# Second block's hybrid mixer: dilated attention moved beside the input projection, and its RMS factors on eight numbers per token

## The chip, the core and the metric

The kernel runs on one NeuronCore of one Trainium2 chip. The metric is the device time of one execution in microseconds (us). Everything is in float32; products that need it are made from a rounded high part and a low part of each operand.

## The reference, cut to what matters

Two model blocks run one after the other over 512 tokens of width 1024. The second block's mixer takes the normed input `h`, projects it, and feeds two mixers whose outputs are joined and projected back:

```python
def hybrid_mixer(h, w_in, gate_bias, g_q, g_k, g_mh, w_out):
    proj = h @ w_in                      # mq, mk, mv, mo, mg, aq, ak, av
    hm = bidirectional_mlstm(mq, mk * 64 ** -0.5, mv, gates of mg)      # 4 heads, both directions
    hm = rms_norm(hm, g_mh) * sigmoid(mo)
    qa = partial_rope(rms_norm(aq, g_q), pos) * 64 ** -0.5              # 8 heads of 64
    ka = partial_rope(rms_norm(ak, g_k), pos)
    ha = dilated_attention(qa, ka, av)   # three bands, dilations 1, 4, 16, merged by their log-sum-exp
    return concatenate([hm, ha]) @ w_out
```

The kernel makes the three bands as one softmax whose weights are multiplied by a table `CM` (how many of the three bands hold a key) and masked by a table `CB`.

## The kernel before, in words

A program is a list of steps. Each engine walks the list in the order in which the steps were added and issues the part that the step has for it, with semaphore waits in front. So on every engine an instruction that waits holds back all that was added behind it. The order of the list is written by hand, with Python generators that are advanced by turns.

`mixer_hybrid` has three stages.

**Projection.** `w_in_2` is taken in 25 chunks of 128 columns (`MQ` 2, `MK` 2, `MV` 4, `MO` 4, `MG` 1, `DQ` 4, `DK` 4, `DV` 4; `D` is the dilated attention, `M` the mLSTM). A chunk is 24 dense matmuls of 512 tokens (`ProjMM`, function `dense`, L192 to L194) into one PSUM bank. ACT copies the bank out (`Evac`). The next chunk's weights are split into a high part on ACT (L179) and a low part on DVE (L184) meanwhile. Small follow-up steps of earlier chunks are generators in the list `lag`; after each chunk's matmuls each of them is advanced by one part. For a `DQ` or `DK` chunk (`normed_rope`, class `NormedRope`) the parts are: square on ACT; a TensorE product with a block of ones that puts each head's sum of squares on all its 64 partitions (L2194), a root on ACT (L2209), a reciprocal of 128x512 on DVE (L2216) and the scaling (L2219); then the rotation (L2198 and three DVE operations); then the split into high and low parts (`HiLo`). A `DV` or `MV` chunk is turned to token-major (`Turn`, L1187). The gate chunk `MG` starts the gates of the mLSTM, and then eight `MlBroadcast` steps (L2431, L2432) which put a running maximum on all partitions, copied by ACT into `MB` (L2439). `MO` chunks leave their bank through a Sigmoid.

**Two mixers side by side.** After `Begin` the generators `mlstm` and `dilated` are advanced by turns.

`dilated` treats 16 pairs `q`, a pair being two heads and 128 queries, in the order (query block, head pair). Its steps for a pair are: `DilScore` (six score matmuls and two mask matmuls into banks 4 and 5, then on DVE a maximum per bank, L2806, then on ACT an Exp per bank into `PP`, L2816); `DilCount` (DVE multiplies with `CM` and sums, L2837); twice `DilTrans`, once for each bank of the pair (four transposes into a bank, L2858, and the copy of that bank by ACT into `PT`, L2865); `DilPV` (L2888). After four pairs come `DilDen` and `DilQuot` (L2937), the division. `DilTrans` takes its PSUM bank so:

```python
        self.b = 3 if u % 2 and 3 in w.ptfree else 6
        self.bankfree = w.ptfree[self.b]
```

and `w.ptfree` holds only bank 6 until the mLSTM gives bank 3 away, late.

`mlstm` treats 16 units (head, key block): `MlExp` (four Exps on ACT, and the three matmuls of the scores, L2505 to L2507), `MlProd` (two multiplications on DVE, L2529), `MlSum` (L2555, L2560). Behind the units comes a chain of small steps: `MlDen`, `MlInverse`, `MlSpread`, `MlQuot`, `MlSquare`, `MlRoot`, `MlRootInverse`, `MlFactor`, `MlOut`, and `MixSplit` of each head, in which DVE, ACT and TensorE hand work to each other.

**Output projection.** `out_products`, with the same dense matmuls on the split mixer output.

Of the kernel before, what the change touches and what calls it, by code (L numbers as in the profile page):

```python
# [1072 lines left out]
class ProjMM(Step):  # L1073


    def __init__(self, pr, parts):
        self.pr, self.parts = pr, parts
        one = len({p.ch for p in parts}) == 1
        self.order = [(p, k) for p in parts for k in range(8)] if one else [
            (p, k) for at in (0, T) for k in range(8) for p in parts if p.c0 == at]  # L1080
        for p, k in self.order:
            if k == 7:
                p.done = p.u.used = pr.P.s["group"].next()
# [155 lines left out]
class Mix:  # L1239


    def __init__(self, MIX, MH, ML):
        self.MIX, self.MH, self.ML = MIX, MH, ML
        self.hi, self.lo, self.order = {}, {}, []


class MixSplit(Step):
# [8 lines left out]
    def scalar(self, act):  # L1256
# [3 lines left out]
        for k in self.ks:  # L1260
            act.e.activation(mix.MH[:, k, :], mix.MIX[:, k, :], ACT.Copy).then_inc(mix.hi[k].sem, 1)

    def vector(self, dve):
        mix = self.mix
        for k in self.ks:
            dve.wait_ge(*mix.hi[k])
            dve.e.tensor_tensor(mix.ML[:, k, :], mix.MIX[:, k, :], mix.MH[:, k, :].bitcast(F32),
# [3 lines left out]
class OutMM(Step):  # L1271
# [11 lines left out]
    def tensor(self, pe):  # L1283
# [4 lines left out]
        for i, k in enumerate(ms.order):  # L1288
            pe.wait_ge(*ms.hi[k])
            pe.wait_ge(*ms.lo[k])  # L1290
            dense(pe, self.P.banks[self.b], u, slice(k * 128, (k + 1) * 128), (ms.MH[:, k, :], ms.ML[:, k, :]), True,
# [872 lines left out]
class NormedRope(Step):  # L2164


    def __init__(self, pr, part, st, tiles):
# [5 lines left out]
        elif part == 1:  # L2173
            self.b, self.free = pr.sidebank()
            self.rsfree = tiles.rsfree
            st["sum"] = tiles.sqfree = s["side_mm"].next()
            st["root"] = pr.sidefree[self.b] = s["nr_act"].next()
            st["inv"] = s["rope"].next()
            st["scaled"] = tiles.rsfree = s["rope"].next()
# [8 lines left out]
    def tensor(self, pe):  # L2188
        P, st, ti = self.P, self.st, self.tiles
        if self.part == 1:  # L2190
# [9 lines left out]
    def scalar(self, act):  # L2200
# [5 lines left out]
        elif self.part == 1:  # L2206
            act.wait_ge(*st["sum"])
            act.wait_ge(*self.rsfree)
            act.e.activation(ti.RS, P.banks[self.b], ACT.Sqrt, scale=1.0 / 64, bias=P.EPSC).then_inc(st["root"].sem, 1)  # L2209

    def vector(self, dve):
        P, st, ti = self.P, self.st, self.tiles
        x = st["x"]
        if self.part == 1:
            dve.wait_ge(*st["root"])
# [3 lines left out]
            dve.e.scalar_tensor_tensor(x, x, st["gain"], ti.RS, ALU.mult, ALU.mult).then_inc(st["scaled"].sem, 1)  # L2219
        elif self.part == 2:  # L2220
# [9 lines left out]
class RopeTiles:  # L2230
    def __init__(self, SQ, RS, TM, RT, PR, landed, gained):
        self.SQ, self.RS, self.TM, self.RT, self.PR, self.landed, self.gained = SQ, RS, TM, RT, PR, landed, gained
        self.sqfree = self.rsfree = self.tmpfree = NONE
# [15 lines left out]
class Mlstm:  # L2249


    def __init__(self, P, Q, K, V, O, G, UT, OH, MIX, lent, kept):
# [9 lines left out]
        room = lambda places: [P.over_ring(f"ROOM{i}{part}", [128, 2, T], F32, part + i * 4096)[:, half, :]  # L2262
                               for i in places for part in (0, NUNIT * 4096) for half in range(2)]
        self.MB, kept = room(lent), room(kept)
# [9 lines left out]
    def tiles(self, ctx, QH, QL, KH, KL):  # L2274
# [3 lines left out]
        self.A = sb("A", [128, 4, T])  # L2278
        self.RH = sb("RH", [36, T], F32R)
# [134 lines left out]
class MlBroadcast(Step):  # L2414


    def __init__(self, m, pr, h, d):
        self.m, self.h, self.d = m, h, d
        self.b, self.free = pr.sidebank()
        self.split = m.mgsplit  # L2420
        self.spread = m.P.s["side_mm"].next()
        self.done = pr.sidefree[self.b] = m.P.s["ml_act"].next()
# [11 lines left out]
    def scalar(self, act):  # L2434
        m = self.m
        act.wait_ge(*self.spread)
        for t in m.lent:
            act.wait_ge(*t)
        act.e.activation(m.MB[self.d * 4 + self.h], m.P.banks[self.b], ACT.Copy).then_inc(self.done.sem, 1)  # L2439
# [288 lines left out]
class MlOut(Step):  # L2728
# [8 lines left out]
    def vector(self, dve):  # L2737
# [4 lines left out]
        dve.wait_ge(*self.scaled)  # L2742
# [1330 lines left out]
```

## Time and profile before

| what | us |
|---|---|
| median of 3 runs | 3217.79 (3216.38 to 3219.81) |
| span of the profiled execution, first to last instruction | 3213.4 |
| TensorE busy in it | 3123.6 (97%) |
| VectorE busy | 1911.2 (59%) |
| ScalarE busy | 1046.4 (33%) |
| mean granted TensorE clock | 0.985 of 2.4 GHz |

The profile gives the span of its execution and no other time of it; what lies around the span is inside the runs' time only. An engine's busy time hides its waits, so the stages are read one by one: the projection is 2465 to 2628 us of the span, the two mixers side by side 2629 to 2792 us, and the dense matmuls of the output projection start at 2792 us. The matmuls' ends are modelled, so the distance from one start to the next is the better duration.

### The profile page before, as it was taken

To read this page: it belongs to the slowest core of one execution; us is meant where nothing else is said; L and a number is where in the kernel's file an instruction comes from. 1 tells how busy PE (TensorE), PEld (TensorE's weight loads), DVE (VectorE), ACT (ScalarE), POOL (GpSimd) and SP (SyncE) were. 2 spreads that over 40 slices of the span, in tenths; PEclk is the share of its full clock that TensorE was granted. 3 is DMA by queue.
4 is the path that set the end of the run, shared out by engine and by line. 5 is a ranking of instruction groups with operands and counts; after the bars stand their busy time and mean duration, and the time that the engine had idled before them with its cause. 6 is when DMAs were issued, how large, how long until landed. Compare 5 with 4: busy or idle time off the path is not lost.

```text
span 3213.4 us, 37101 instructions
## 1 busy us (share of the span) xinstructions
PE 3123.6 (97%) x15003; PEld 2512.4 (78%) x15014; DVE 1911.2 (59%) x2753; ACT 1046.4 (33%) x1516; POOL 10.2 (0%) x23
## 2 busy tenths in 40 slices
PE   8999999998899999999999999999999998899998
PEld 7888888776678888788877888788887764578887
DVE  7876555645675554766657554566665565574444
ACT  4212222335442222422235222332224444442222
POOL 0000000000000000000000000000000000000000
PEclk9999999999999999999999999999999999899999
DMA  6433332210033443256532443235551220133231
GB/s 231 141 118 127 147 126 81 68 46 11 2 132 127 158 153 131 79 192 214 196 107 79 150 158 138 79 118 202 185 189 59 78 59 1 47 119 104 92 99 53
DMA packets 102996, 369.21 MB, mean 115 GB/s; under 512 B 11374, under 2 KB 12670, under 8 KB 102572
## 3 DMA queue, kind: packets, MB, share of 16 engines
q1 hardware_dynamic: 101788, 362.14, 33.0%
q0 software_dynamic: 1040, 4.71, 0.4%
q8 instruction: 120, 1.97, 0.3%
q14 instruction: 48, 0.39, 0.0%
HBM read 364.71 MB, written 2.10 MB: 114 GB/s over the span
## 4 chain that ended last, share of the span: by engine, by line
PE 88%; DVE 7%; ACT 3%; issue 1%; DMA 1%; SPq 0%; POOL 0%; DVEq 0%; ACTq 0%; POOLq 0%
PE ps L192 25%; PE ps L194 25%; PE ps L193 25%; PE ps L196 4%; PE ps L197 2%; DVE SQ L614 1%; PE ps L499 1%; DVE WL L184 1%; DVE HL L603 1%; DVE XT L1037 1%; DVE RAW L1499 0%; PE ps L2888 0%; PE ps L2858 0%; PE ps L2788 0%; PE ps L2555 0%
## 5 line engine op out<-in xcount | busy, mean ns | idle before, releaser
L192 PE MATMUL ps<-HH,WH 128*128 128x512 f32 x2400 | 945.3, 394 | 4.0 <-ACT S L914 2.2
L194 PE MATMUL ps<-HH,WL 128*128 128x512 f32 x2400 | 935.1, 390 | 0.0
L193 PE MATMUL ps<-HL,WH 128*128 128x512 f32 x2400 | 934.5, 389 | 0.0
L179 ACT ACTIVATE WH<-RAW 128x1024 fp32r<-128x1024 f32 x456 | 459.2, 1048 | 632.0 <-PE ps L194 361.8
L184 DVE TENSOR_TENSOR WL<-RAW,WH 128x1024 fp32r<-128x1024 f32 x456 | 542.8, 1220 | 73.5 <-ACT WH L179 73.2
L192 PEld LDWEIGHTS ps<-HH,WH 128*128 128x128 f32 x2400 | 450.7, 188 | 107.5 <-issue 9.5
L193 PEld LDWEIGHTS ps<-HL,WH 128*128 128x128 f32 x2400 | 450.9, 188 | 95.2 <-issue 3.8
L194 PEld LDWEIGHTS ps<-HH,WL 128*128 128x128 f32 x2400 | 450.5, 188 | 95.4
L1037 DVE SCALAR_TENSOR_TENSOR XT<-ps,DER,XT 128x512 f32<-128x512 f32 x512 | 346.6, 683 | 246.6 <-PE ps L194 231.8
L192 PE MATMUL ps<-GH,WH 128*128 128x512 f32 x1056 | 414.1, 392 | 4.8 <-DVE GL L945 4.8
L194 PE MATMUL ps<-GH,WL 128*128 128x512 f32 x1056 | 411.2, 389 | 0.0
L193 PE MATMUL ps<-GL,WH 128*128 128x512 f32 x1056 | 411.0, 389 | 0.0
L943 DVE TENSOR_TENSOR S<-S,ps 128x512 f32<-128x512 f32 x128 | 88.0, 687 | 513.9 <-PE ps L194 513.9
L918 ACT ACTIVATE GH<-S 128x512 fp32r<-128x512 f32 x128 | 80.9, 632 | 625.2 <-DVE S L943 625.2
L305 DVE SCALAR_TENSOR_TENSOR DUMP<-RAW,CC 128x1024 bf16<-128x1024 f32 x200 | 244.4, 1222 | 12.4 <-DVE DUMP L305 0.5
L192 PEld LDWEIGHTS ps<-GH,WH 128*128 128x128 f32 x1056 | 198.2, 188 | 49.9 <-issue 7.5
L194 PEld LDWEIGHTS ps<-GH,WL 128*128 128x128 f32 x1056 | 198.2, 188 | 42.0
L193 PEld LDWEIGHTS ps<-GL,WH 128*128 128x128 f32 x1056 | 198.4, 188 | 39.3 <-issue 0.7
L196 PE MATMUL ps<-HC,WH 128*128 128x512 f32 x424 | 152.1, 399 | 0.0
L945 DVE TENSOR_TENSOR GL<-S,GH 128x512 fp32r<-128x512 f32 x128 | 88.6, 693 | 97.0 <-ACT GH L918 97.0
L914 ACT ACTIVATE S<-ps 128x512 f32<-128x512 f32 x128 | 76.0, 594 | 201.8 <-PE ps L194 201.6
L197 PE MATMUL ps<-HC,WL 128*128 128x256 f32 x424 | 118.8, 280 | 0.0
(382 smaller groups left out, 2627.0 us busy)
## 6 DMA issues: line engine op xcount, KB each, us to landing
RAW<-in_w_modt SPq DMA_DIRECT2D x200, 512.0 KB, 5.0
RAW<-in_ffn_wi SPq DMA_DIRECT2D x182, 512.0 KB, 5.0
RAW<-in_w_gu SPq DMA_DIRECT2D x90, 512.0 KB, 4.5
RAW<-in_ffn_wo SPq DMA_DIRECT2D x88, 512.0 KB, 4.6
RAW<-in_w_in SPq DMA_DIRECT2D x44, 512.0 KB, 3.6
RAW<-in_w_down SPq DMA_DIRECT2D x44, 512.0 KB, 4.2
RAW<-in_w_out SPq DMA_DIRECT2D x16, 512.0 KB, 4.5
STG<-in_w_modt SPq DMA_DIRECT2D x10, 512.0 KB, 12.7
```

What stands on the lines that cost most here:

```text
L179: act.e.activation(u.hi, u.ld.view, ACT.Copy).then_inc(u.hi_done.sem, 1)
L184: dve.e.tensor_tensor(u.lo, u.ld.view, u.hi.bitcast(F32), ALU.subtract).then_inc(u.lo_done.sem, 1)
L192: pe.e.matmul(out, wh, x[0], start=first, stop=False)
L193: pe.e.matmul(out, wh, x[1], start=False, stop=False)
L194: m = pe.e.matmul(out, wl, x[0], start=False, stop=last)
L196: pe.e.matmul(out, wh, x, start=first, stop=True, skip_group_check=not first)
L197: m = pe.e.matmul(out[:, 0:TC], wl, x[:, 0:TC], start=False, stop=True, skip_group_check=True)
L305: dve.e.scalar_tensor_tensor(self.dump, self.view, 1.0, tile[:, :], ALU.mult, ALU.mult, accum_out=self.P.DOT[:, self.row % 2, j, self.f:se ...
L918: act.e.activation(gh, s, ACT.Copy).then_inc(self.hi[n].sem, 1)
L943: dve.e.tensor_tensor(s, s, F.SX[:, :] if n else out, ALU.mult).then_inc(self.mul[n].sem, 1)
L945: dve.e.tensor_tensor(gl, s, gh.bitcast(F32), ALU.subtract).then_inc(self.lo[n].sem, 1)
L1037: dve.e.scalar_tensor_tensor(x, o, P.mod_g(F.mi, d, j), x, ALU.mult, ALU.add).then_inc(w.evac[d, n][i].sem, 1)
```

## The change

- The order of the projection's chunks becomes, for i = 0 to 3, `DQ+i`, `DK+i`, `DV+i` and `MG` (i = 0) or `MV+i-1`; then `MV+3`, `MQ`, `MK`, and `MO` last.
- `projection` gets a hook, `between`: after each chunk but the first two (which are made as one job) it advances the generator `dilated` two times. `dilated` waits, in the list, until `DQ` and `DK` of its head pair are split.
- The 16 pairs are ordered (head pair, query block). The steps of a pair come in another order, in two pieces: `DilScore(q)`, `DilTrans(2q-2)`; then `DilDen`, `DilTrans(2q-1)`, `DilPV(q-2)`, `DilQuot`, `DilCount(q)`. Both pieces stand right behind each other in the projection.
- The projection has two banks instead of four (0, 1) and two side banks (2, 3); the attention keeps 4 to 7, and `w.ptfree` holds bank 6 alone.
- `NormedRope` has four parts. The sums of squares are taken as [128 tokens, 8] by four matmuls with two moving columns each; ACT takes Ln and Exp of these 8 numbers per token (half the exponent negated), DVE refines them by three small operations, and eight matmuls with a broadcast stationary operand spread them to a bank, from which the scaling reads. The 3.35 us reciprocal is gone. `LogExpTable` loads one activation table set ahead.
- The eight `MlBroadcast` steps leave the projection and stand at the start of `mlstm`, on banks 0 to 2. The sigmoid of `MO` becomes a step `MlSigmoid` behind `MlDen`.
- What is left beside `mlstm` is `dilated_end`: the `MixSplit` of the four dilated chunks.

```diff
@@ class NormedRope: tensor, scalar, vector @@
-            pe.e.matmul(P.banks[self.b], ti.PR[:, 128:256], ti.SQ, start=True, stop=True).then_inc(st["sum"].sem, 1)
+            for n in range(4):
+                m = pe.e.matmul(P.banks[self.b][:, 2 * n:2 * n + 2], ti.SQ[:, n * 128:(n + 1) * 128], ti.PR[:, 128:256:64],
+                                start=True, stop=True)
+            m.then_inc(st["sum"].sem, 1)
         elif self.part == 2:
+            pe.wait_ge(*st["inv"])
+            pe.wait_ge(*self.free)
+            for n in range(4):
+                for h in range(2):
+                    rs = ti.RS[:, st["at"], 2 * n + h:2 * n + h + 1].broadcast_to([128, 64])
+                    m = pe.e.matmul(P.banks[self.b][64 * h:64 * h + 64, n * 128:(n + 1) * 128], rs, P.ID, start=True,
+                                    stop=True, skip_group_check=True)
+            m.then_inc(st["spread"].sem, 1)
+        elif self.part == 3:
...
-            act.e.activation(ti.RS, P.banks[self.b], ACT.Sqrt, scale=1.0 / 64, bias=P.EPSC).then_inc(st["root"].sem, 1)
+            act.e.activation(r, P.banks[self.b][:, 0:8], ACT.Ln, scale=1.0 / 64, bias=P.EPSC).then_inc(self.ln.sem, 1)
+            act.wait_ge(*self.ln)
+            act.e.activation(r, r, ACT.Exp, scale=-0.5).then_inc(st["root"].sem, 1)
...
-            dve.e.reciprocal(ti.RS, ti.RS).then_inc(st["inv"].sem, 1)
-            dve.wait_ge(*st["inv"])
+            dve.e.scalar_tensor_tensor(v, ss, EPS * 64, r, ALU.add, ALU.mult).then_inc(self.prod.sem, 1)
+            dve.wait_ge(*self.prod)
+            dve.e.scalar_tensor_tensor(v, v, -0.5 / 64, r, ALU.mult, ALU.mult).then_inc(self.half.sem, 1)
+            dve.wait_ge(*self.half)
+            dve.e.scalar_tensor_tensor(r, v, 1.5, r, ALU.add, ALU.mult).then_inc(st["inv"].sem, 1)
@@ class Program: projection @@
                     evac(p)
+                    if len(chs) == 1 and between:
+                        between()
+                        between()
@@ mixer_hybrid @@
-                pr = Proj(self, h, (0, 1, 2, 3), (4, 5, 6, 7))
+                pr = Proj(self, h, (0, 1), (2, 3))
...
-                order = [DQ, DV, MG, DV + 1, DQ + 1, DV + 2, DV + 3, DQ + 2, MQ, MQ + 1, DQ + 3, MK, MK + 1]
+                order = []
                 for i in range(4):
-                    order += [DK + i, MV + i]
-                order += list(range(MO, MG))
-                self.projection(pr, a["w_in_2"], order, lambda ch: [(0, T)], evac, lag)
+                    order += [DQ + i, DK + i, DV + i, MG if i == 0 else MV + i - 1]
+                order += [MV + 3, MQ, MQ + 1, MK, MK + 1] + list(range(MO, MG))
+                self.projection(pr, a["w_in_2"], order, lambda ch: [(0, T)], evac, lag, between=lambda: next(steps, None))
@@ dilated @@
         for q in range(last + 2):
-            if 1 <= q <= last:
-                self.add(DilCount(w, q - 1))
             if q < last:
+                while w.pairs[q][0] not in w.qsplit or w.pairs[q][0] not in w.ksplit:
+                    yield
                 self.add(DilScore(w, q))
-                yield
             if 1 <= q <= last:
                 self.add(DilTrans(w, 2 * q - 2))
-                yield
+            yield
+            if 1 <= q <= last:
                 if q % 4 == 0:
                     self.add(DilDen(w, q // 4 - 1))
                 self.add(DilTrans(w, 2 * q - 1))
...
                 self.add(DilPV(w, q - 2))
                 if q % 4 == 1:
                     self.add(DilQuot(w, q // 4 - 1))
-                yield
+            if q < last:
+                self.add(DilCount(w, q))
+            yield
@@ mlstm @@
         split(0)
-        yield
+        done = [NONE] * 3
+        for h in range(4):
+            for d in range(2):
+                done.append(self.add(MlBroadcast(m, h, d, done[-3])).done)
+            if h % 2:
+                yield
...
         self.add(MlDen(m, last.done))
+        self.add(MlSigmoid(m))
```

## Rows read from the trace of the kernel before

**Rows 1.** Busy time by stage; columns: stretch, length, PE, PEld, DVE, ACT, POOL, granted clock

```profile
2465.10:2628.20 163.10, 162.43 (x684) 123.13 (x684) 101.87 (x101) 69.34 (x99) 3.15 (x6) 1.00 0.27 79
2629.10:2704.95 75.85, 69.56 (x338) 32.29 (x344) 40.39 (x86) 42.05 (x95) 0.00 (x0) 1.00 0.00 1
2704.95:2792.20 87.25, 67.85 (x399) 39.44 (x404) 54.59 (x110) 35.79 (x60) 0.00 (x0) 0.78 0.09 29
```

**Rows 2.** Timeline of ACT, evacuations of the projection's last two chunks

```profile
2622.80 0.60 ACT L1131 ACTIVATE MIX<-ps 128x512 f32<-128x512 f32 x1 [3.89 <-PE ps L194]
2628.24 0.60 ACT L1131 ACTIVATE MIX<-ps 128x512 f32<-128x512 f32 x1 [4.84 <-PE ps L194]
```

**Rows 3.** Timeline of all engines, one step of the attention (start, length)

```profile
2742.45 0.49 PE L2788 MATMUL ps<-KH,QH 64*128 64x512 f32 x2
...
2744.07 1.02 PE L2673 MATMUL ps<-A,OH 128*4 128x512 f32 x2
2744.18 1.29 DVE L2806 TENSOR_REDUCE NM<-ps 128x1 f32<-128x512 f32 x2 [2.02 <-PE ps L2788]
2744.91 1.29 ACT L2816 ACTIVATE PP<-ps,NM 128x512 f32<-128x512 f32 x2 [1.48 <-DVE NM L2806]
2745.03 1.09 PE L2858 MATMUL ps<-K,PP 128*128 128x128 f32 x8
...
2746.05 1.09 PE L2888 MATMUL ps<-PT,DVt 128*64 128x128 f32 x16
2746.09 1.08 ACT L2865 ACTIVATE PT<-ps 128x512 f32<-128x512 f32 x2
```

**Rows 4.** Chain of waits, projection: one product with the ones

```profile
2604.20 0.86 PE ps L2194 x2
```

**Rows 5.** Timeline of PE: one broadcast in the projection; the nearest to two-column sums

```profile
2515.73 0.49 PE L2431 MATMUL ps<-MGH,SEL 4*128 4x512 f32 x1
...
2516.38 0.66 PE L1187 MATMUL ps<-K,SQ 128*128 128x128 f32 x4
...
2821.64 0.50 PE L764 MATMUL ps<-K,ACC 128*128 128x1 f32 x4
2822.01 0.47 PE L192 MATMUL ps<-MH,WH 128*128 128x512 f32 x1
```

**Rows 6.** Groups by line, both stages (count, then busy us, mean ns, idle before)

```profile
L2216 DVE RECIPROCAL TMP<-TMP 128x512 f32<-128x512 f32 x8 | 26.8, 3353 | 24.4 <-ACT TMP L2209 24.4
...
L2209 ACT ACT_TABLE_LOAD x2 | 2.6, 1283 | 0.0
...
L2937 PE MATMUL ps<-XT,K 128*64 128x512 f32 x16 | 4.8, 605 | 0.4 <-DVE XT L2913 0.4
...
L2602 DVE RECIPROCAL G<-G 36x128 f32<-36x128 f32 x4 | 3.8, 946 | 0.1
L2640 DVE TENSOR_TENSOR ROOM<-ROOM,ps 128x512 f32<-128x512 f32 x8 | 5.1, 680 | 0.0
```

**Rows 7.** Timeline of PE: one unit of the mLSTM, from its scores to the next work

```profile
2666.95 0.49 PE L2505 MATMUL ps<-MQH,MKH 64*128 64x512 f32 x1
...
2670.08 0.50 PE L2788 MATMUL ps<-KH,QH 64*128 64x512 f32 x2
```

**Rows 8.** Timeline of DVE: one head's output steps and its split, twice

```profile
2776.99 0.69 DVE L1267 TENSOR_TENSOR ML<-MIX,MH 128x512 fp32r<-128x512 f32 x1 [1.27 <-ACT MH L1261]
...
2779.76 0.69 DVE L1267 TENSOR_TENSOR ML<-MIX,MH 128x512 fp32r<-128x512 f32 x1 [0.69 <-ACT MH L1261]
```

**Rows 9.** Timeline of PE: starts behind an idle stretch (length in brackets)

```profile
1306.68 1.11 PE L713 MATMUL ps<-SA,K 128*128 128x512 f32 x1 [2.02 <-DVE SA L417]
...
2706.84 0.63 PE L2858 MATMUL ps<-K,PP 128*128 128x128 f32 x4 [1.90 <-ACT G L2585]
```

**Rows 10.** Busy time and granted clock of the stretches behind those two

```profile
1307.20:1310.50 3.30, 3.30 (x8) 1.96 (x7) 3.30 (x5) 1.89 (x3) 0.00 (x0) 0.54 0.14 21
...
2706.84:2710.00 3.16, 3.00 (x27) 1.84 (x28) 2.28 (x6) 0.60 (x1) 0.00 (x0) 1.00 0.02 5
```

More of the change, by code:

```diff
@@ L1242, in __init__ @@
     def __init__(self, MIX, MH, ML):
-        self.MIX, self.MH, self.ML = MIX, MH, ML
+        views = lambda t: t if isinstance(t, list) else [t[:, k, :] for k in range(8)]
+        self.MIX, self.MH, self.ML = MIX, views(MH), views(ML)
         self.hi, self.lo, self.order = {}, {}, []
@@ L2414, with __init__ @@
 class MlBroadcast(Step):
[L2417 to L2422, printed above, removed]
+    def __init__(self, m, h, d, before):
+        self.m, self.h, self.d, self.b = m, h, d, (2 * h + d) % 3
+        self.split, self.free = m.mgsplit, before
+        self.spread = m.P.s["ml_mm"].next()
+        self.done = m.P.s["ml_act"].next()
         m.bcast[h, d] = self.done
@@ L2434, in scalar, with __init__ @@
     def scalar(self, act):
+        m, h = self.m, self.h
+        act.wait_ge(*self.spread)
+        act.e.activation(m.MB[self.d * 4 + self.h], m.P.banks[self.b], ACT.Copy).then_inc(self.done.sem, 1)
+class MlSigmoid(Step):
+    def __init__(self, m):
+        self.m = m
+        m.opened = [m.P.s["ml_gate"].next() for _ in range(4)]
+    def scalar(self, act):
         m = self.m
[L2436 to L2439, printed above, removed]
+        for h in range(4):
+            act.e.activation(m.O[:, h, :], m.O[:, h, :], ACT.Sigmoid).then_inc(m.opened[h].sem, 1)
 class MlMask(Step):
@@ L2815, in scalar @@
                 act.wait_ge(*w.trans[u - 4].turned)
-            act.e.activation(w.PP[:, u % 4, :], w.P.banks[4 + par], ACT.Exp,
+            else:
+                for t in w.freed:
+                    act.wait_ge(*t)
+            act.e.activation(w.PP[u % 4], w.P.banks[4 + par], ACT.Exp,
                              bias=w.NM[:, s, hs:hs + 1]).then_inc(self.exp[par].sem, 1)
@@ L2872, in __init__ @@
         self.w, self.q = w, q
-        self.n, self.j = w.pairs[q]
-        self.ready = [w.trans[2 * q + par].done for par in range(2)]
+        self.j, self.n = w.pairs[q]
+        self.ready = [w.trans[2 * q + par].done for par in range(2)] + [w.turned[self.j]]
         self.done = w.P.s["dil_mm"].next()
@@ L3326, in follow, with projection @@
         lag.append(g)
-    def projection(self, pr, w, chunks, segs_of, evac, lag, beside=None, depth=1):
+    def projection(self, pr, w, chunks, segs_of, evac, lag, beside=None, depth=1, between=None):
         def job(chs):
@@ L3848, in dilated, with dilated_end @@
                     self.add(DilQuot(w, q // 4 - 1))
-                yield
+            if q < last:
+                self.add(DilCount(w, q))
+            yield
+    def dilated_end(self, w, steps, mix):
+        for _ in steps:
+            yield
+        for k in range(4, 8):
+            self.add(MixSplit(self, mix, [k], [w.quot[k - 4].done]))
+            yield
     def plan(self):
```

173 lines of the change are left out of this document (96 added, 77 removed).

## The prediction

> **What bounds the kernel now.** I read the busy time by stage first [rows 1]. In the projection TensorE is busy 162.4 of 163.1 us at full clock: a chunk costs what its matmuls cost, and the reader is to see that ACT (69 us) and DVE (102 us) have room there. In the two stretches of the mixers TensorE is idle 6.3 of 75.9 us and then 19.4 of 87.3 us, and the granted clock of the second is 0.78. So the place where there is something to win is the second stretch, 2705 to 2792 us, and everything that the change sends into the projection costs its full TensorE time, since nothing there is free. A dense chunk is 5.44 us from one evacuation to the next [rows 2].
>
> **The attention's matmuls, moved.** They cost TensorE the same wherever they stand. From the start of one step's scores to what follows is 1.62 us (2742.45 to 2744.07), the transposes of both banks of a pair take 1.02 us (2745.03 to 2746.05), and the product with V 1.02 us (eight matmuls; half of the row's records would be 0.5) [rows 3]. The divisor's spread is at most 4.8 us for all four [rows 6]. Sum: 16 x 1.62 + 16 x 1.02 + 16 x 1.02 + 4.8 = 63.3 us more in the projection. The list shows where they fall: `DQ`, `DK` of head pair 0 are split at the sixth chunk, pair q = 0 starts there, the splits of the later head pairs are ready at chunks 9, 13 and 17 (counted from 0), exactly when q = 4, 8, 12 ask for them, so there is one pair per chunk without a hole and q = 17 ends two chunks before the end. All 63.3 us lie in the projection.
>
> **A new wait inside each step.** This is the term that decides. Follow one step behind a chunk. TensorE: scores of q, transposes of 2q-2 into bank 6, transposes of 2q-1 into bank 6 again, product q-2, next chunk. The second transposes wait until ACT has copied bank 6 away. But ACT's list has, before that copy, the two Exps of q, these wait for the two maxima of q on DVE, and these for the scores of q. In the rows of one step [rows 3] the scores end at 2744.07, the maxima start at 2744.18, the Exps at 2744.91, and the first copy can only start at 2746.09, behind them. It takes about 0.54 us (half of 1.08), so bank 6 is free at about 2746.7. The first transposes would be over at 2744.07 + 0.51 = 2744.6. TensorE would stand still for 2.1 us. Before the change the two `DilTrans` of a pair were added a turn apart, with mLSTM matmuls in between (0.95 us of them stand in this row, before the transposes), and the Exps of a pair a turn earlier still. After it, both pieces of the step stand right behind each other and behind the still waiting transposes stand the product and the whole next chunk. q = 1 to 15 have this wait: 15 x 2.1 = 31.5 us. In six of these chunks DVE still has a rotation and a turned chunk to copy before the maxima, which makes the wait some 0.5 us longer: 3.0 us. For q = 16 there are no scores and only the copy is waited for, 0.7 us. Sum 35.2 us. Bounds: nothing, if something hides it, and 50 us (3.3 us per step) if DVE and ACT are found busy with the weights' split each time.
>
> Who else waits: `DilCount` is behind the Exps on DVE and ends in the next chunk, before the next transposes need it. The split of the next chunk's weights is added before a chunk's matmuls and has the 5.4 us of that chunk; it is not late. ACT's copies and Exps, moved, add 16 x (1.29 + 1.08) us to a 69 us load, DVE's maxima and counts about as much: neither becomes the bound, each chunk now lasting about 11 us.
>
> **Norm factors.** The reciprocals, 26.8 us of DVE [rows 6], and their roots lie beside the matmuls: they cost nothing now, but for one wait of 0.7 us at the second chunk (163.1 less 162.4). On TensorE: eight products of 0.86 us go, 6.9 us [rows 4]. For the sums of squares (four float32 matmuls, eight records, two columns) the nearest row is 0.37 us for four records with one column [rows 5], so 0.74 us each, 5.9 us in all (0.37 if they pair up: 3.0). The spread is eight matmuls of 128 columns on half the array's width, like the product with V [rows 3]: 1.02 us each, 8.2 us (at best half, 4.1). The eight broadcasts leave: 0.65 us each [rows 5], 5.2 us. Sum: -6.9 + 5.9 + 8.2 - 5.2 - 0.7 = +1.3 us. The small operations on ACT and DVE (under 0.3 us each) have a chunk's time each. The new second side bank is enough: no part waits for a bank that a slower one of the same chunk holds for more than 0.3 us. The weight loads on SP's queue and the tables on POOL's are the same in number; a chunk lasts longer than before, so they come no later.
>
> In a sentence of its own: the Trainium skill, "ScalarE: Activation LUTs", section "Table sets: the hidden batching unit", says that one set holds both Exp and Ln, so the preloaded set should serve the whole projection; no row here shows it. If it did not, loads would come back into ACT's list, and that is the fourth rival below.
>
> **The mLSTM alone.** One unit costs TensorE 3.13 us from start to start of what follows [rows 7]; units with less wide sums cost 0.2 less, so 3.0. DVE (two products, a quarter of the masks) and ACT (four Exps) need less than 2 us each, and a unit's exponentials only wait for the sums two units before, so TensorE sets the pace. The start: splits of q and k, eight broadcasts whose copies take 0.6 us each on ACT, two splits of `dilated_end` between them, two masks, the first Exps and products: 11.2 us (estimate, 8 to 13) until the first sum. Then 15 x 3.0 + 1.5 for four heads' changes + 2.1 for the last sum. 59.8 us. The chain behind it: floor and denominator on ACT 1.9 (the idle stretch before 2706.84 [rows 9]); four inverses, 3.8 [rows 6] and 1.0 for their maxima; split and first spread 2.5; twelve DVE operations of 0.64 (5.1/8 [rows 6]), 7.8; square, its sum, root, refinement, split and the first factor 8.8, of which the filler matmuls at low clock are a part; four heads at 2.77, each with the turn to ACT and back [rows 8], 11.1; the split of the first output weights 1.6. Sum 38.5 us (30 to 42). `MlSigmoid` lies beside the inverses. Together 98.3 us, against 2792.2 - 2628.2 = 164.0 before: -65.7 us. The clock: TensorE idles for most of the chain and at the start, and where before the clock rose just before the output matmuls it will now be low when they begin. 3.5 us (0 to 7). So -62.2 us.
>
> **The clock in the projection.** The question is whether idle stretches of 2.1 to 2.7 us let it fall. Behind the 2.02 us stretch that ends at 1306.68 the granted clock is 0.54 of 2.4 GHz for 3.3 us, though dense matmuls go on; behind 1.90 us it stays at 1.00 [rows 9, 10]. In the whole trace, idle stretches of TensorE between 1.6 and 1.9 us never lowered it when matmuls stood around them (six), and those between 1.99 and 2.6 us did in six cases of seven. 2.1 us is just beyond the boundary. I take 10 of 15 steps, each with 3.4 us at 1.2 GHz, in which half is lost: 17 us (0 to 51, the latter if each falls and takes twice as long to rise, as it did in the stage of small matmuls).
>
> The Trainium skill, "TensorE: Matmul & The Clock Gate", section "HAM oscillation — how this bites in real kernels", would let only idle gaps clearly longer than these lower the clock. By that rule the 17 us would be 0. The row of 1306.68 disagrees, and I go by the row; the rule is the second rival.
>
> **Sum.** +63.3 + 35.2 + 1.3 in the projection, -62.2 behind it, +17 of clock = +54.6 us. On the profile's span of 3213.4 us that is 3268.0. The runs' median lies 4.4 us above the span, for what is around it; it moves with it: 3217.8 + 54.6 = 3272.4, I say 3272 us.
>
> **Rivals.**
>
> First, the other side: the wait for bank 6 is hidden, a step costs only its matmuls, and the clock holds. Then the sum is 54.6 - 35.2 - 17 = +2.4, and -12 with the terms that have a low end there (spreads -4.1, sums of squares -2.9, start -3.2, clock behind the stage -3.5). About 3213 us. It decides from the point where a step's idle is under about 0.1 us. For it: ACT has room and the copy is short. Against it: the order in ACT's list is fixed, and the rows of one step show each link [rows 3].
>
> Second: the wait is there but the clock holds: 54.6 - 17 = +37.6, 3255 us. For it: the 1.90 us stretch, only 0.2 shorter. Against it: the 2.02 us one.
>
> Third: nearly every step loses the clock, and for longer, because scores and products use half of the array or less: 17 becomes some 45, 3300 us.
>
> Fourth, that the set loaded ahead does not stay: a load (1.3 us [rows 6]) before some Exps, on the very chain that TensorE waits for, for the eight chunks in which a Ln stands: +10 us, 3282 us.
>
> **Chances.** The forecast 0.48; hidden wait 0.12; clock holds 0.20; third 0.12; fourth 0.05; something else at the start or in the chain, slower still, 0.03. Below the range lies nearly all of the first rival, above it part of the third: 3238 to 3300. A measurement of this kernel can tell about 0.2%, 6.4 us, from no change. Of the first rival somewhat more than half lies below that: faster 0.07, same 0.05, all the rest slower, 0.88.
>
> **What would show it.** In the changed kernel: each pair of transposes from q = 1 on in two groups with some 2.1 us of TensorE idle between them, released by ACT's copy; ACT's Exps waiting for DVE's maxima in each step; a chunk pitch of 11 to 12 us from the sixth chunk on; projection about 263 us plus the clock; granted clock below 1.00 in patches there; from the last projection matmul to the first output matmul about 100 us. No reciprocal of 128x512. If the two groups of transposes stand together, or if the pitch is near 9.5 us, I am wrong at the second term; if the wait is there and the clock reads 1.00, at the last.

## The result, and the profile after

The changed kernel takes 3280.09 us (median of 4 runs, 3277.9 to 3284.87), the kernel before 3217.11 us on the same chip (4 runs, 3216.38 to 3219.81). The ratio is 1.0199, 95% interval 1.0186 to 1.0211: 63 us slower. The profiled execution has a span of 3278.4 us and a mean granted clock of 0.980.

Busy time by stage, as in [rows 1]; first the projection, then the mLSTM alone, up to the first matmul of the output projection:

```profile
2468.30:2753.75 285.45, 248.62 (x1356) 181.20 (x1372) 128.50 (x229) 98.28 (x163) 3.15 (x6) 0.94 0.17 53
2753.75:2855.05 101.30, 75.56 (x236) 31.63 (x237) 50.52 (x90) 48.59 (x103) 0.00 (x0) 0.79 0.00 0
```

The projection is 122.3 us longer (285.4 against 163.1), the part behind it 62.7 us shorter (101.3 against 164.0). TensorE, which had 0.7 us of idle time in the projection before, now shows 36.8 us (285.45 less 248.62). The waits of TensorE in that stage name the reason (engine and line, what it waited for, us in all, times, longest):

```profile
PE ps L2906 <- ACT ROOM L2913: 33.6, 16, 2.5
PE ps L2840 <- issue: 2.5, 16, 0.2
PE ps L2202 <- ACT TMP L2224: 0.6, 1, 0.6
```

L2906 is the transposes, L2913 the copy of bank 6. The row with "issue" is no stop of TensorE: L2840 is the two mask matmuls of each pair, and of these 32 the trace holds 16 records. In r1 below, whose trace holds all 32, the second one starts 0.66 us behind the scores' first record, exactly as the recorded one does here, and no such row appears. So the real idle time is 34.3 us.

One step of the attention, all engines, against [rows 3]:

```profile
2719.76 0.39 PE L2833 MATMUL ps<-KH,QL 64*128 64x512 f32 x2
2720.09 0.66 PE L2906 MATMUL ps<-K,ROOM 128*128 128x128 f32 x4
2720.20 1.29 DVE L2851 TENSOR_REDUCE NM<-ps 128x1 f32<-128x512 f32 x2 [6.88 <-PE ps L2833]
2720.93 1.28 ACT L2864 ACTIVATE ROOM<-ps,NM 128x512 f32<-128x512 f32 x2 [1.77 <-DVE NM L2851]
...
2722.11 0.59 ACT L2913 ACTIVATE ROOM<-ps 128x512 f32<-128x512 f32 x1
...
2722.84 0.63 PE L2906 MATMUL ps<-K,ROOM 128*128 128x128 f32 x4 [2.10 <-ACT ROOM L2913]
```

Read it from the top: scores end, maxima start 0.1 us later, the Exps 0.7 us after that, and the copy, ready to run since the first transposes ended at 2720.7, starts at 2722.11, behind the Exps in ACT's list. The second transposes stand 2.10 us. Twelve steps show 2.09 or 2.10 us, three show 2.54, and the last one 0.83. Before, the same pair of transposes stood in one row without a gap [rows 3].

The granted clock behind three of these waits (ending at 2566.70, 2722.84 and 2554.18):

```profile
2566.70:2570.10 3.40, 3.40 (x22) 2.70 (x23) 2.01 (x6) 1.54 (x2) 0.00 (x0) 0.55 0.00 0
2723.70:2727.10 3.40, 3.40 (x21) 2.75 (x18) 1.98 (x4) 1.35 (x2) 0.00 (x0) 0.54 0.00 0
2554.20:2557.60 3.40, 3.40 (x28) 2.75 (x29) 1.28 (x4) 2.06 (x3) 0.00 (x0) 1.00 0.02 5
```

0.55 and 0.54 are the lower level, 1.2 GHz; 22 and 21 matmul records fit in where 28 do at 1.00. Ten of the fifteen steps have such a patch, 34 us in all, so 17 us are lost.

Lines of the new norm factors (groups; count, busy us, mean ns, idle before) and the one table load of the stage:

```profile
L2211 PE MATMUL ps<-K,RS 128*64 128x128 f32 x128 | 8.7, 279 | 0.0
L2202 PE MATMUL ps<-PR,TMP 128*128 128x2 f32 x64 | 8.1, 249 | 0.6 <-ACT TMP L2224 0.6
```

```profile
L2270 ACT ACT_TABLE_LOAD x1 | 1.3, 1283 | 0.0
```

And the waits of TensorE in the mLSTM alone, the two largest:

```profile
PE ps L192 <- ACT WH L179: 10.7, 1, 10.7
PE ps L2667 <- DVE RL L1209: 7.9, 1, 7.9
```

### The profile page after: what moved, and what is told of

Same layout as the page of the kernel before. It is cut to its first block, busy times and chain, and to the rows that moved or that the text cites. A ratio compares the mean times of both kernels' runs of the same rounds, so it can differ in the third digit from the quotient of the medians.

```text
span 3278.4 us, 37495 instructions
## 1 busy us (share of the span) xinstructions
PE 3148.0 (96%) x15174; PEld 2527.6 (77%) x15190; DVE 1890.1 (58%) x2769; ACT 1040.8 (32%) x1522; POOL 10.2 (0%) x23
## 4 chain that ended last, share of the span: by engine, by line
PE 86%; DVE 8%; ACT 4%; issue 1%; DMA 1%; SPq 0%; POOL 0%; DVEq 0%; ACTq 0%; POOLq 0%
PE ps L192 24%; PE ps L193 24%; PE ps L194 24%; PE ps L196 4%; PE ps L197 2%; DVE SQ L614 1%; PE ps L2936 1%; DVE WL L184 1%; DVE HL L603 1%; PE ps L2602 1%; ACT ROOM L2864 1%; PE ps L499 1%; DVE XT L1037 0%; DVE RAW L1500 0%; DVE DUMP L305 0%
```

## The experiments

Stages are compared by their lengths: from the projection's first dense matmul to its last, from there to the first output matmul, and from there to the end of the span. The projection's first matmul lies between 2463.1 and 2468.3 us in the traces of all these kernels, though nothing differs before it, so a stage's length says more than a span. All in us, worked out from the start and end of those matmuls:

| kernel | projection | mixers behind it | both | rest |
|---|---|---|---|---|
| before | 163.1 | 164.0 | 327.1 | 421.2 |
| changed | 285.4 | 101.3 | 386.7 | 423.4 |
| r1 scores last | 240.6 | 99.2 | 339.8 | 423.0 |
| r2 filler | 269.9 | 100.3 | 370.2 | 423.1 |
| r3 norm alone | 172.4 | 164.6 | 337.0 | 421.2 |
| r4 two banks | 256.2 | 100.2 | 356.4 | 423.1 |
| r5 four in the chain | 220.0 | 126.1 | 346.1 | 423.1 |
| r6 four in the units | 218.4 | 125.5 | 344.0 | 422.8 |
| r7 wide norm | 237.6 | 101.4 | 339.0 | 424.6 |
| r8 three in the chain, wide norm | 217.7 | 118.6 | 336.3 | 424.0 |
| r9 wide, pairs first | 229.7 | 99.5 | 329.3 | 424.3 |
| r10 narrow, pairs first | 243.9 | 102.3 | 346.2 | 423.0 |
| r11 fillers | 229.7 | 108.1 | 337.8 | 422.3 |
| r12 turn later, fillers | 225.2 | 101.9 | 327.2 | 422.6 |

**r1: the order within a step.** The changed kernel with the scores behind both transposes, so that the copy stands ahead of the Exps in ACT's list. The product with V moves too, from behind the second transposes to between the two:

```diff
+            while q < last and (w.pairs[q][0] not in w.qsplit or w.pairs[q][0] not in w.ksplit):
+                yield
-            if q < last:
...
-                self.add(DilScore(w, q))
             if 1 <= q <= last:
                 self.add(DilTrans(w, 2 * q - 2))
-            yield
+            if q >= 2:
+                self.add(DilPV(w, q - 2))
             if 1 <= q <= last:
                 self.add(DilTrans(w, 2 * q - 1))
...
+            yield
+            if q < last:
+                self.add(DilScore(w, q))
```

> The changed kernel with the attention's steps in another order: first transposes, product with V, second transposes, then the scores; the work is the same. Theory A (the second transposes wait for ACT's copy of bank 6, which stands behind the Exps of the scores, and the idle stretch lowers the clock): TensorE's 33.6 us of waits for that copy go to under 3 us, the granted clock in the projection is 1.00, 3229 us (3222 to 3240). Rival B (the attention's chain through DVE and ACT is too long for one chunk in any order): the wait appears somewhere else, time stays above 3265.

Measured: 3229.07 us (3226.9 to 3235.25), ratio 1.0042 (1.0028 to 1.0056). TensorE's waits for the copy fall from 33.6 to 2.8 us and the lower clock in the projection from 34.1 to 6.8 us: 30.8 + 13.7 = 44.5 of the 46.9 us by which the two stages are shorter. By the medians 51 of the 63 us of loss are this one order. No run parts its two moves. The last step of the changed kernel has no scores, and its second transposes wait 0.83 us with no product between; 15 steps like that would be 12 us (estimate), so the later scores bring most of the gain and the product between the transposes the rest.

**r2: the wait filled.** The changed kernel with four matmuls of 128x256, results unused, ahead of each pair's second transposes:

```diff
...
+        if self.u % 2:
+            pe.wait_ge(*self.fill)
+            for _ in range(4):
+                pe.e.matmul(P.banks[self.fb][:, 0:256], P.ID, P.K[:, 0:256], start=True, stop=True)
         pe.wait_ge(*self.bankfree)
```

> The changed kernel with four filler matmuls (1.7 us) on a free side bank before the second transposes of each pair; they change no result. Theory A, its second half (the lowered clock costs 17 us by itself): the wait stays, filled, and the clock stays 1.00 in the projection: 3263 us (3258 to 3268). Rival (the low patches cost nothing, because other things are waited for in them): 3278 to 3284, whatever the clock reads.

Measured: 3259.93 us (3258.89 to 3261.51), ratio 1.0135 (1.012 to 1.015). A step of it on TensorE, and the projection's clock:

```profile
2518.56 1.89 PE L2909 MATMUL ps<-K 128*128 128x256 f32 x8
2520.73 0.66 PE L2912 MATMUL ps<-K,ROOM 128*128 128x128 f32 x4 [0.28 <-ACT ROOM L2919]
```

```profile
PE ps L2912 <- ACT ROOM L2919: 4.4, 15, 0.3
```

The second transposes start 2.66 us behind the first (2.75 in the changed kernel), so nearly as late, but TensorE works until then, and no patch of the lower clock is left in the projection. It is 15.5 us shorter, against the 17 us that the patches cost; of the 20.1 us between the two spans 3.3 are only an earlier start of the stage. So the clock term is separate from the wait and about as large as said.

**r3: the norm factors alone**, put into the kernel before (the `NormedRope` and `LogExpTable` of the diff, nothing else).

> The kernel before with nothing of the change but the norm factors on eight numbers per token (four parts of NormedRope, one table set loaded ahead). My sum, with the sizes of the profile after: eight sums at 0.9 us and eight spreads at 1.0 in place of eight products of 0.86 us, 0.7 us of a wait gone: +8 us, 3225 us (3221 to 3229). Rival (the reciprocals' 27 us of DVE were felt somewhere): at or under 3217.

Measured: 3224.62 us (3220.29 to 3228.99), ratio 1.0022 (1.0013 to 1.0031). The projection:

```profile
2463.85:2636.29 172.44, 171.77 (x860) 133.70 (x860) 79.17 (x117) 63.33 (x104) 3.14 (x6) 1.00 0.24 75
```

It is 9.3 us longer, with DVE's load down from 102 to 79 us: the change relieves an engine that nobody waited for and pays on the one that is full.

**r4: two banks for the transposes**, in the changed kernel's own order. One of the two side banks goes to them:

```diff
-        self.ptfree, self.ofree = {6: NONE}, NONE
+        self.ptfree, self.ofree = {6: NONE, 3: NONE}, NONE
...
-                pr = Proj(self, h, (0, 1), (2, 3))
+                pr = Proj(self, h, (0, 1), (2,))
```

> The changed kernel, its order of steps kept, with bank 3 given to the second transposes and only bank 2 left to the side products of the projection. Theory A: the second transposes start at once, no wait for the copy; the side products now wait for each other's bank in three chunks of four, about 13 us in all; clock 1.00: 3242 us (3232 to 3252). Rival (it is not the bank but the late copy itself that holds TensorE, in the product with V): no gain, above 3270.

Measured: 3246.24 us (3244.34 to 3247.1), ratio 1.0091 (1.0076 to 1.0106). The wait for the copy is gone, others came in its place, all for the one side bank that is left:

```profile
PE ps L2202 <- DVE MIX L2248: 4.2, 4, 1.4
PE ps L1187 <- DVE DKt L2248: 3.7, 4, 0.9
PE ps L2211 <- DVE TMP L2253: 3.5, 4, 0.9
PE ps L1187 <- DVE TMP L2253: 2.6, 3, 0.9
```

That is 14.0 us. 33.6 - 14.0 = 19.6, and 10.2 us of clock (34.1 less 13.7 us at the lower level, halved): 29.8 of the 30.3 us that the stages gave back.

**r5 and r6: four pairs left where TensorE has holes.** r1, with the hook advancing the attention only 30 times; the four pairs of the last head pair run beside the chain behind the last unit (r5), or beside the units (r6: no turns held back).

```diff
+                early = (next(steps, None) for _ in range(30))
...
-                self.projection(pr, a["w_in_2"], order, lambda ch: [(0, T)], evac, lag, between=lambda: next(steps, None))
+                self.projection(pr, a["w_in_2"], order, lambda ch: [(0, T)], evac, lag, between=lambda: next(early, None))
@@ dilated_end, ahead of the rest of steps: the first two splits, and 16 turns held back (none in r6) @@
+        for k in range(4, 6):
+            self.add(MixSplit(self, mix, [k], [w.quot[k - 4].done]))
+            yield
+        for _ in range(16):
+            yield
...
```

> Kernel: the order of r1 (scores last in a step), and the four pairs of head pair 3 (q = 12 to 15) are not run beside the projection but beside the chain behind the mLSTM's last unit, where TensorE idles (40 us long from the last sum to the first output matmul in the changed kernel, TensorE busy for about a quarter). Theory A (matmuls moved into the projection cost their full time; those beside the chain are free as long as the chain doesn't wait for them): the projection gets 4 x 3.9 = 15.8 us shorter, the chain gets longer by about half of that, since its small DVE and ACT steps wait for the Exps and counts of the pairs: 3229 - 15.8 + 8 = 3221 us, 3214 to 3228. Rival B (the chain is held up by each pair as long as the pair's own maxima, Exps, counts and copies on DVE and ACT take, 4.9 us per pair): 3229 - 15.8 + 4 x 4.9 = 3233 us.

> As r5, but the four pairs run beside the mLSTM's units, where TensorE is itself the bound (2.9 to 3.1 us per unit). Theory A: TensorE's time is only moved from one full stage to another, so about the same as r1, 3229 us (3224 to 3234). Rival B (a unit leaves TensorE idle between its parts, which pairs would fill): 3215 us or less. If A holds and r5 is below r6, then where a pair stands decides, by whether TensorE idles there.

Measured: r5 3236.95 us (3233.65 to 3240.45), ratio 1.0062 (1.0048 to 1.0075); r6 3234.71 us (3231.91 to 3237.1), ratio 1.0055 (1.0041 to 1.0069). My theory was wrong for both. In r5 the projection got 20.6 us shorter, but the stage behind it 26.9 us longer. More than four pairs' work had moved: a pair is spread over three steps, and the trace has the scores of four pairs, the transposes of five and the products with V of six behind the projection, in r6 too. That is why the projection gained more than the 15.8 us expected. What it cost is still more than it gained, by 6.3 us; the rival had said 3.8. The wait of 7.9 us in the chain was not filled but replaced:

```profile
PE ps L2906 <- DVE ROOM L2885: 11.1, 4, 5.0
PE ps L2552 <- DVE A L2576: 2.2, 1, 2.2
```

L2885 is the multiplication with `CM`: a pair is itself a chain over DVE and ACT, and with nothing else between its parts TensorE waits for each. The 11.2 us before the output matmuls stayed as well, since no pair was left by then. r6 gained 22.2 us in the projection and paid 26.3 us for the same work; 5.1 us of it are waits for the copy of bank 6. Without them its theory, that work between two full stages is only moved, would have held.

**r7: the norm factors wide.** r1 with one product with the ones, Ln and Exp on 128x512, and the three refinements on 128x512; `V` shares its place with the rotation's temporary.

```diff
-            for n in range(4):
-                m = pe.e.matmul(P.banks[self.b][:, 2 * n:2 * n + 2], ti.SQ[:, n * 128:(n + 1) * 128], ti.PR[:, 128:256:64],
-                                start=True, stop=True)
+            pe.e.matmul(P.banks[self.b], ti.PR[:, 128:256], ti.SQ, start=True, stop=True).then_inc(st["sum"].sem, 1)
...
-            dve.e.scalar_tensor_tensor(x, x, st["gain"], P.banks[self.b], ALU.mult, ALU.mult).then_inc(st["scaled"].sem, 1)
+            dve.e.scalar_tensor_tensor(x, x, st["gain"], r, ALU.mult, ALU.mult).then_inc(st["scaled"].sem, 1)
```

> Kernel: the order of r1, and the norm factors not on 8 numbers per token: one product with the ones (0.86 us), Ln and Exp on 128x512, and the three refinements on 128x512 on DVE. Taken away from TensorE: four two-column sums (0.91 us in the changed kernel) and the eight-matmul spread (1.02 us), of each of the eight chunks: 8 x (0.91 + 1.02 - 0.86) = 8.6 us. Theory A (the norm part costs TensorE's time, and nothing else): 3229 - 8.6 = 3220.5 us, 3217 to 3225. Rival B (the narrow form is worth what it costs, because three wide operations of about 0.7 to 1.3 us on DVE per chunk hold up the attention's maxima and the weights' low part): 3229 us or slower.

**r8: r5 and r7 together.**

> r5 and r7 together. Theory A (the two gains lie in different stages and add up): r5 - 8 us, about 3213 us, that is a little faster than the kernel before (3217.5). Rival B (they overlap, or the wide operations on DVE hold up the chain): as r5, 3221 us, no faster than before.

Measured: r7 3227.68 us (3227.24 to 3229.66), ratio 1.0035 (1.0022 to 1.0047); r8 3229.21 us (3228.04 to 3231.43), ratio 1.004 (1.0027 to 1.0052). r7 was to gain 8.6 us and gained 3.0 in the projection. Of r7, TensorE in the projection:

```profile
PE ps L2889 <- ACT ROOM L2896: 9.3, 6, 2.7
```

The wait for the copy is 6.5 us more than in r1: the wide Ln and Exp, and the wide operations on DVE, stand ahead of it. With it both theories hold a part: the narrow form costs TensorE about 9 us, and the wide one gives most of that back through the order of the lists. r8 is 7.7 us faster than r5, but it isn't r5 and r7 added up. The wide form has one part less, so the splits are ready earlier, and the same 30 advances get one pair further: the trace has 13 pairs' scores in the projection (r5: 12) and three behind it. Of the 9.8 us between the two traces' stages 7.5 lie in the mixers' stage, which differs by that pair alone. So r8 says nothing on whether the two gains add up.

**r9 and r10: the attention's pieces first.** Behind a chunk's matmuls the two pieces of the attention's step, then the small follow-up steps and the evacuation; r9 with the wide norm factors (r7), r10 with the narrow ones (r1).

```diff
+                    if len(chs) == 1 and between:
+                        between()
+                        between()
                     if p.c0 == 0:
                         self.advance(lag)
                     evac(p)
-                    if len(chs) == 1 and between:
-                        between()
-                        between()
```

> r7 (scores last in a step, wide norm factors), and in addition the two pieces of the attention's step stand ahead of a chunk's small follow-up steps (norm, turns, rotation) and of its evacuation, not behind them. Theory A (in r7 the Ln and Exp of 128x512 on ACT and the wide operations on DVE stand ahead of the first transposes' copy and of the maxima, and this is what TensorE's 10 us of idle are): the idle goes to under 1 us, 9 us less, and with it the clock patches of 6.8 us, 3.4 us less: 3227.7 - 12.4 = 3215 us (3212 to 3220), a little faster than the kernel before. Rival B (the wait only changes its place: the follow-up products on TensorE now wait for ACT and DVE behind the Exps): 3225 to 3230 us.

> The same order with the narrow norm factors of the change (r1 with the pieces ahead of the follow-up steps). Theory A: r1's 3.4 us of idle and 3.4 us of clock go: 3229.1 - 6.8 = 3222 us (3219 to 3226); against r9 it then shows what the narrow form costs TensorE when nothing waits: 7 us (8.6 by the records' durations). Rival B (the spread, now further behind the Exps on ACT, waits): 3229 us or more.

Measured: r9 3219.45 us (3217.5 to 3225.26), ratio 1.0011 (1.0002 to 1.002); r10 3236.95 us (3236.79 to 3237.63), ratio 1.0062 (1.0048 to 1.0076). r9 came near its expectation, r10 missed it by 15 us. The stage of r9, and what TensorE waited for in r9 and in r10:

```profile
2464.17:2693.91 229.74, 222.94 (x1181) 160.33 (x1196) 140.65 (x229) 104.71 (x163) 3.14 (x6) 0.99 0.21 66
```

```profile
PE ps L1187 <- DVE UT L2431: 3.0, 1, 3.0
...
PE ps L2889 <- ACT ROOM L2896: 0.8, 1, 0.8
```

```profile
PE ps L1187 <- DVE TMP L2253: 4.3, 2, 2.1
...
PE ps L2211 <- DVE UT L2448: 1.9, 1, 1.9
```

In r9 the copy's wait went, and one new wait came where three side products share two banks. The narrow form has a product more per chunk, so it meets that wait more often. r10's projection is 14.2 us longer than r9's: 9.3 us is left when the waits (7.0 and 3.8 us) and the lower clock (6.8 and 3.4 us, halved) are taken out. That is r3's figure again. r10's own expectation had the waits going to nothing; they rose from 2.8 to 7.0 us instead.

**r11 and r12: fillers in the chain.** r11 is r9 with 28 matmuls of 128x256 behind the last sum and 38 behind the last factor; r12 has 16 and 23, and the turn of the running maxima one chunk later.

```diff
                     self.add(MlMax(m))
                     yield
+                    yield
...
         self.add(MlSigmoid(m))
+        self.add(Busy(self, 16, bank=4))
...
+            if h == 3:
+                self.add(Busy(self, 23, bank=4))
```

> r9, and filler matmuls of 128x256 (0.24 us each at full clock) in the two long idle stretches of the chain behind the mLSTM: 28 behind the last sum (idle 7.9 us) and 38 behind the last factor (idle 10.7 us); their results are not used. Theory A (in that chain the granted clock is low for about 17 and 14 us behind these two stretches, and spreads, squares and the first output matmuls run at half speed because of it): the clock holds, spreads and squares take half of their 12 us less what DVE needs anyway, 4 to 6 us, and the first output matmuls 2.3 us: 8 us faster than r9, 3207 us (3204 to 3212). Rival B (DVE and ACT set the pace of the chain, the clock does not matter there): as r9, or some us slower where fillers run past the idle.

> r9 with two additions. First, the turn of the gates' running maxima (three side products fall into its chunk, on two banks, and TensorE waits 3.0 us there, with a clock patch of 3.4 us behind it) comes one chunk later, where one product fewer is. Second, the fillers of r11 at the size that the idle stretches have: one of them took 0.44 us in r11 (28 of them 12.35 us), not 0.24, so 16 behind the last sum (7.0 of 7.9 us) and 23 behind the last factor (10.1 of 11.2 us). Theory A (a wait removed in a full stage comes back whole with its clock patch; fillers that end before the chain does cost nothing and keep the clock for the squares' sums, 2.9 us, and the first output matmuls, 2.4 us): 3219.5 - 3.0 - 1.7 - 2.9 - 2.4 = 3209.5 us (3207 to 3214), 0.2% faster than the kernel before. Rival B (DVE and ACT set the chain's pace, so the fillers give nothing, and the wait for the turn moves to the next chunk): 3217 to 3220 us, no different from before.

Measured: r11 3229.02 us (3226.32 to 3229.69), ratio 1.0036 (1.0022 to 1.005); r12 3215.74 us (3213.65 to 3219.11), ratio 0.9997 (0.9988 to 1.0006). In r11 I had taken half of a filler's price; of r11 and then of r12:

```profile
2755.88 12.35 PE L499 MATMUL ps<-K 128*128 128x256 f32 x56
```

```profile
2768.64 6.22 PE L2703 MATMUL ps<-A,OH 128*4 128x512 f32 x8
...
2782.28 12.81 PE L499 MATMUL ps<-K 128*128 128x256 f32 x46
2794.74 0.58 PE L192 MATMUL ps<-MH,WH 128*128 128x512 f32 x1
```

28 matmuls are 56 records, 12.35 us for a hole of 7.9. In r12 the first filler fits, but the clock fell behind it all the same (it is low from 2763.7 to 2774.0), and the squares' sums still take 6.22 us. The second filler ran partly at the lower clock and lasted 12.8 us for a hole of 11.2. So fillers gave the chain nothing: that stage is 101.9 us, r9's 99.5. r11 shows how little the clock weighs there: from the first spread to the kernel's own next fillers (`PE L499`, 12 records) the clock is low for 6.8 us in r11 and 11.9 us in r9, and r11 takes 13.35 us where r9 takes 14.17. In the main DVE and ACT set the chain's pace, as the rival said. The first output matmuls ran at full clock, 1.7 us (rest of 422.6 against 424.3). The later turn did what was expected, 4.5 us of the projection. Both runs missed their expectations, 3207 and 3209.5 us, by 22 and 6 us. r12 beats the changed kernel by 64 us and is not told apart from the kernel before: the ratio's interval holds 1. No version here beats both.

## Why the prediction was right

The forecast was 3272 us with +54.6 us; measured are 3280.09 and +63.0. By its own steps:

- **The moved matmuls, +63.3.** What is left of r1's projection (240.6 - 163.1 = 77.5) without its waits for the copy (2.8), clock (3.4) and norm less broadcasts (4.1, next point but one) is 67.2 us; the changed kernel's gives 67.6. From start to start the pairs' own matmuls take 64 us of r1's projection at full clock, about as priced. The other 3 us lie beside them: compared with r3, the small follow-up products take 2.0 us more and the dense matmuls 0.9 us more, now that other matmuls stand next to them. That I had put at nothing.
- **The wait for bank 6, +35.2.** Measured 33.6: twelve of 2.1, three of 2.5 (I had said six longer ones), and 0.83. r1 and r4 take away the cause in two different ways, and the wait goes in both.
- **Norm factors, +1.3.** The term with the largest relative error. r3 shows 9.3 us without the broadcasts' leaving; less 5.2 it is +4.1. The sums of squares take 0.88 to 0.98 us each from start to start, 7.4 us in all, not 5.9, and the wait of 0.7 us at the second chunk did not go, it is 0.6 now (L2202). The reciprocal's leaving gave nothing, as said.
- **The mLSTM alone, -65.7 and 3.5 for the clock.** Measured -62.7. The chain from the last sum to the first output matmul is 40 us (estimated 38.5), the first sum 12.2 us behind the projection (11.2).
- **The clock, +17.** Ten of fifteen steps, 3.4 us each: the trace has exactly the number taken, 34.1 us of lower clock, and r2 gives 15.5 us back. The rival "the wait is there but the clock holds" fell here. That stops of this size can cost the clock was read rightly from the rows. The exact number is luck: it rested on a boundary in the stop's length, and the last section shows that the length alone doesn't decide.
- The rest of the span is 2.2 us longer (3.5 expected for the clock). The lower clock lies over its first matmuls for about 5 us; r9 and r12, with and without that, are 1.7 us apart. The stages' differences add up to 61.8 us, and the profiled spans differ by 65.0; the 3.2 us left are the later start of the projection, which the forecast doesn't have.
- **One sign missed.** The chunk pitch was to be 11 to 12 us; the steps' second transposes are 14.2 us apart on average. 11 to 12 is a bare dense chunk with a pair and its wait, without the chunk's follow-up products and the clock, which the forecast's own sum does contain. The first rival's sum with all its low ends is -11.3, not -12; nothing hangs on it.

The first three points and the clock make 118.0 of the 122.3 us in the projection; the 4.3 us left are the first point's. The mechanism, the wait in each step and its price, was right, and the other terms were each within 4.3 us. Of the rivals, the hidden wait did not come, nor the third; the fourth is excluded by the single table load for the whole stage. The Trainium skill says the same of it, "ScalarE: Activation LUTs", section "Table sets: the hidden batching unit" (one set holds Exp and Ln), and the trace agrees.

**Where the gain of the move went.** r9 and r12, with the wide norm factors, leave out nearly all the waits that the new order brought, and there 16 pairs beside the projection instead of beside the mLSTM take 2.1 and 0.1 us more in the two stages together. The reason is in the mixers' stage. Of before, and of r9:

```profile
2628.20:2792.24 164.04, 137.47 (x738) 71.78 (x749) 94.98 (x196) 78.62 (x155) 0.00 (x0) 0.89 0.05 16
```

```profile
2693.91:2793.42 99.51, 73.00 (x237) 30.81 (x237) 50.63 (x90) 48.56 (x103) 0.00 (x0) 0.82 0.00 0
```

The stage got 64.5 us shorter and TensorE's work in it 64.5 us less. TensorE idles 26.6 us in the first and 26.5 us in the second, but not in the same places. The largest waits of before, and of r9:

```profile
PE ps L2858 <- DVE PP L2837: 9.9, 3, 4.6
```

```profile
PE ps L192 <- ACT WH L179: 11.2, 1, 11.2
PE ps L2650 <- DVE RL L1209: 7.8, 1, 7.8
```

Before, nine of the 16 pairs' scores and twelve of the products with V stood beside the chain behind the last sum. The pairs' matmuls keep TensorE busy for 52 us of its 87.3 us [rows 1], and the largest waits are their own, for the multiplication with `CM` (L2837). With the pairs gone (r9) the chain takes 39.5 us, and its two long holes open. So the pairs had filled the chain's holes and brought their own waits; taken away, they left a stage with as much idle time as before. That the two sums agree so closely is chance. The lower clock weighs the same too (0.11 x 164.0 = 18 us lost, and 0.18 x 99.5 = 18). Work moved from a stage with holes to a full one pays only if the holes shrink.

**Open.** Whether dense chunks (the four of `MO`, needed only at the chain's end) would fill the chain's holes better than pairs was not tried: the mLSTM's tables lie in the weights' places.

## What to carry to other kernels

Before moving work, look at who would use the idle time that it leaves: here TensorE's idle time in the stage left behind was 26.6 us before and 26.5 us after. Where two uses of one bank stand in a step, put the copy that frees it ahead of anything on its engine that waits for the same step's products, and other TensorE work between the two uses; the order of one list was worth 51 us, and a second bank 34. An operation on a relieved engine is no gain when its replacement puts small matmuls on the full one: 26.8 us of reciprocals were exchanged for 9.3 us that counted.

## What the runs showed of the hardware

Idle time alone doesn't say when the clock falls. In the changed kernel stretches of 2.10 us were followed by the lower clock in ten steps of twelve, while the three of 2.54 us, in otherwise the same place, never were. In r1 a shorter one was enough, and the clock stayed low twice as long (the transposes, then the windows behind):

```profile
2520.58 0.63 PE L2906 MATMUL ps<-K,ROOM 128*128 128x128 f32 x4 [1.17 <-ACT ROOM L2913]
```

```profile
2521.50:2528.30 6.80, 6.80 (x19) 4.05 (x18) 3.82 (x7) 3.09 (x5) 0.00 (x0) 0.53 0.01 2
```

The Trainium skill, "TensorE: Matmul & The Clock Gate", section "HAM oscillation — how this bites in real kernels", lets only idle gaps longer than all of these bring the clock down; the traces disagree, and the measurement decides. Nor do the instructions around the gap decide it: r7 and r8 have the same projection until the last pairs, and in it the same two stops of 1.70 us, and behind both the clock fell in r7 and behind neither in r8. What else decides is open.

A float32 matmul with two moving columns is no cheap one: the four of a chunk's sums of squares are eight records, and from their start to the next matmul they take 0.88 to 0.98 us, 0.11 a record, so 0.23 us a matmul. A filler of 256 columns took 0.44 us (28 of them 12.35 us in r11), and half of that, 0.22 us, is an estimate for 128 columns. And dense matmuls at the lower clock start 0.43 us apart (first output matmuls of r9, from 2794.41 to 2794.84) instead of 0.23 (the same ones in r12), fillers too, so a filler must be sized for the clock that it will meet.
